# A two-layer hybrid backbone on one NeuronCore: the last scan group reordered, and seven attention steps placed beside the last projection tiles of the odd layer

## The chip, the cores and the metric

The program runs on one core of one Trainium2 chip. The metric is the device time of one execution in microseconds (us), lower is better. Engines are named as in the profile: PE is TensorE (matrix products), PEld its weight loads, DVE is VectorE, ACT is ScalarE, POOL is GpSimd, SP is SyncE, which here only issues transfers. Each engine works through its own list of instructions in order; the engines meet at semaphores.

## The reference, cut to what matters

256 latent tokens and 256 context tokens of width 1024 pass through two layers in fp32. The even layer mixes by a Fourier part and a bidirectional state-space scan (four groups of six heads, four chunks of 128 tokens); the odd layer mixes by attention. Each layer ends with a squared-ReLU MLP. The two places that the change touches:

```python
# even layer: per group of heads, over chunks of 128 tokens, in both directions
y = C_chunk @ entering_state * decay + (B C^T * decay_mask) @ (x * dt)

# odd layer
qw, kw, vw, qn, kn, vn = split(u @ w_in)           # 8 window heads over 2 shared k/v heads, 8 neighbourhood heads
q, k = rms_norm(q) * g, rms_norm(k) * g            # per head of 64
qw, kw = axial_rope(qw), axial_rope(kw)            # latent tokens, window heads alone
p = softmax([scores over 256 latent and 256 context keys, (window: sink)] + mask or bias)
out = concat(p_window @ vw, p_neighbour @ vn) @ w_out
```

## The kernel before, in words

**Order.** `script()` (L162) writes one list of steps, and every engine's block walks this same list and emits its own share of each step. So the order of the list is the order of work on every engine, and a step moved in it moves on all of them. `job()` (L376) gives every matrix product a PSUM bank (of 8) and keeps which semaphore count frees the bank's previous user; PE waits for that count (`emptied`) before it writes.

**Projection tiles.** A product by 128 columns of a weight is a step `gemm`. Every fp32 weight tile is loaded by SP into a ring of 4 slots, split by ACT into a rounded part (`high`, L1023: `w_hi`) and by DVE into the rest (`low`, L1393: `w_lo`), both done at the step of the tile two places ahead (`AHEAD = 2`). A tile is then 24 matmuls (8 pieces of the contraction by hi·hi, lo·hi, hi·lo), over 512 columns for k and v and 256 for q.

**Odd layer before.** `ODD` (L90) lists 18 tiles: v.0 to v.4, kw.0, kn.0 to kn.3, qw.0 to qw.3, qn.0 to qn.3. After tile n come, on the following places of the list: `hstat` of tile n-1 (PE sums squares over each head in a bank of `B_AUX`, ACT takes ln and exp), `hnorm` of tile n-2 (five DVE operations, L1821 to L1829; the second, L1823, is the last reader of the `hstat` bank), `rot` of tile n-3 for window heads (PE permutes, three DVE operations L1835 to L1838), `vtok` (PE transposes v, ACT copies), and `dup` (two PE products and two DVE copies that lay each shared key head twice, seven tiles behind kw.0).

**Attention before.** 16 steps i, for 8 pairs of heads t and two query halves. A step is: `S` (PE, four matmuls into two neighbouring banks), `max` (DVE adds mask or bias, reduces, negates; L1859 to L1870), `exp` (ACT, two exponentials that free the two banks, L1370, and for the window heads one for the sink, L1373), `scale` (DVE reciprocal and two multiplications, L1882 and L1886), `PT` (PE transposes the probabilities, ACT copies them, L1381), `O` (PE, L2386), and for every second step `ohi` (ACT) and `olo` (DVE) split the output. `S(0)` stands ahead of the last tile, everything else of attention behind it. `S` alternates between banks 4, 5 and 0, 1. Then come `grow` (transposes, L2199) and the tiles `outO`.

**Scan, last group before.** For each chunk: `seg` (ACT six Relu L1252 and one Exp L1255, DVE one product L1681, once for each direction f and b), `yoff` (PE L2164, DVE L1692, a sum L1697), `y` (PE: 24 products L2177, which wait for both `seg`, then six L2181 that add the `yoff` result and wait for DVE), `yt` (DVE adds the chunk to `mixF`, L1708). Beside them run the z tiles (DVE `gating`, L1405) and `mixsplit` f = 0 to 7 (DVE L1732 and L1734, or ACT for f below 2), which write the hi and lo operands of the pair of tiles outA 0 and outA 1. That pair (`pair_product`, L1920, 48 matmuls) waits at each of its eight pieces for the `mixsplit` of the piece.

Of the kernel before, what the change touches and what calls it, by code (L numbers as in the profile page):

```python
# [14 lines left out]
ALU = mybir.AluOpType  # L15
# [72 lines left out]

ODD_AT = {"qn": (768, SEQ), "kn": (1280, T), "qw": (0, SEQ), "kw": (512, T)}
ODD = [(kind, int(i), ODD_AT[kind][0] + P * int(i), ODD_AT[kind][1]) if kind != "v" else ("v", int(i), 640 if i == "0" else 1664 + P * int(i), T)  # L90
       for kind, i in (q.split(".") for q in ("v.0 kw.0 kn.0 kn.1 v.1 qw.0 qw.1 v.2 qw.2 qw.3 kn.2 qn.0 qn.1 kn.3 qn.2 qn.3 v.3 v.4").split())]
# [70 lines left out]
def script():  # L162
# [131 lines left out]
    for n in range(len(ODD) + 3):  # L294
        if n == len(ODD) - 1:
            s.append(("S", 0))
        if n < len(ODD):
            gemm(*ODD[n][:2])
        if n == len(ODD) - 1:
            s.append(("max", 0))  # L300

        behind = lambda back: [o[:2] for i, o in enumerate(ODD) if max(i, 1) == n - back]
        for back, stage in ((1, "hstat"), (2, "hnorm"), (3, "rot")):
            s.extend((stage,) + o for o in behind(back) if o[0] != "v" and (stage != "rot" or o[0][1] == "w"))
        s.extend(("vtok", o[1]) for o in behind(1) if o[0] == "v")
        s.extend(("dup",) for o in behind(7) if o[0] == "kw")
    n = len(ATTN)
    for j in range(-1, n + 1):
        for kind, i in (("S", j + 2), ("ohi", j - 2), ("max", j + 1), ("scale", j), ("olo", j - 2), ("exp", j + 1), ("PT", j), ("O", j - 1)):
            if kind in ("ohi", "olo"):  # L310
                if i >= 0 and i % 2 == 1:
                    s.append((kind, i // 2))
            elif 0 <= i < n and (kind, i) != ("max", 0):
                s.append((kind, i))
# [26 lines left out]
def trunk(nc, x, ctx, w_mod, vectors, w_ff1, w_ff2, w_in_even, w_dt, w_out_even, w_in_odd, rpb_na, w_out_odd,  # L341
# [45 lines left out]
    for st in steps:  # L387
# [93 lines left out]
        elif k == "cb":  # L481
            job(st, B_AUX[0])
        elif k == "hstat":
            job(st, B_AUX[n_aux % 2], freed=("hv_done", nk))
            n_aux += 1
        elif k == "yoff":
            for i, (q, none) in enumerate((("f", SCAN_F[0]), ("b", SCAN_B[0]))):
# [4 lines left out]
        elif k == "rot":  # L492
            job(st, B_Y)
        elif k == "dup":
            job(st + (0,), B_TR, freed=("kd_done", 1))
            job(st + (1,), B_TR, freed=("kd_done", 2))
        elif k == "S":
            for par in range(2):
                job(st + (par,), (B_SEG, B_GEMM[0])[st[1] % 2] + par)
        elif k == "PT":  # L500
            for par in range(2):
                job(st + (par,), (B_TR, B_AUX[0])[par], freed=("pT_done", 2 * st[1] + par + 1))
        elif k == "O" and st[1] % 2 == 0:
            t = st[1] // 2
            job(("Opair", t), (B_Y, B_AUX[1])[t % 2], freed=("split_done", 5 * KT + t + 1), filled=("pv_done", 4 * t + 4))
# [8 lines left out]
    with ExitStack() as stack:  # L514
# [505 lines left out]
        def _(act):  # L1020
# [39 lines left out]
            for st in steps:  # L1060
# [321 lines left out]
                elif k == "ohi":  # L1382
                    b = jobs[("Opair", st[1])][0]
                    act.wait_ge(*filled(("Opair", st[1])))
                    nc.scalar.activation(a_hi[:, st[1], 0:SEQ], ps[:, b, 0:SEQ], ACT.Copy).then_inc(signal(ohi_done), 1)


        @block.vector
        def _(dve):
# [51 lines left out]
            for st in steps:  # L1441
# [395 lines left out]
                    dve.wait_ge(*latest())  # L1837
                    v.tensor_tensor(x_, rp[:, 0, :], rp[:, 1, :], ALU.add).then_inc(signal(rope_done), 1)  # L1838
                elif k == "dup":
                    for q in range(2):  # L1840
                        b = jobs[st + (q,)][0]
                        dve.wait_ge(*filled(st + (q,)))
                        v.tensor_copy(kdup[:, q, :], ps[:, b, :]).then_inc(signal(kd_done), 1)
                elif k == "max":
                    i = st[1]
                    t, qt = ATTN[i]
# [57 lines left out]
        def _(pe):  # L1904
# [42 lines left out]
            for st in steps:  # L1947
# [391 lines left out]
                    mm(ps[:, b, 0:SEQ], cuts["perm"], ktile(*st[1:])[:, 0:SEQ], start=True, stop=True).then_inc(filling(st), 1)  # L2339
                elif k == "dup":  # L2340
                    pe.wait_ge(rope_done, rot_n[("rot", "kw", 0)] + 1)
                    for q in range(2):
                        b = jobs[st + (q,)][0]
                        if free_before[st + (q,)]:
                            pe.wait_ge(*emptied(st + (q,)))
                        mm(ps[:, b, :], cuts[f"dup{q}"], kT[:, 0, :], start=True, stop=True).then_inc(filling(st + (q,)), 1)
# [114 lines left out]
```

## Time and profile before

| what | us |
|---|---|
| runs, median of 3 (lowest to highest) | 1212.22 (1210.06 to 1213.14) |
| profiled execution, its own time | 1210.93 |
| its span, first to last instruction | 1209.1 |
| mean granted PE clock, share of full | 0.997 |
| busy: PE, PEld, DVE, ACT, POOL | 1162.3, 933.2, 841.0, 617.0, 84.4 |

The odd layer's tiles and attention stand from 855 to 993 us of the span, the last scan group from 341 to 394 us. Times in the rows are from the span's start. A busy share of PE near 1 means that matrix work follows without a gap; where it falls, another engine, or a semaphore, is late.

### The profile page before, as it was taken

What the parts mean: (1) busy time and instruction counts of PE and PEld (TensorE: products, weight loads), DVE (VectorE), ACT (ScalarE), POOL (GpSimd) and SP (SyncE); (2) the same over time, 40 slices, a digit from 0 to 9 for tenths busy, and PEclk for the clock granted to TensorE, in tenths of its full rate; (3) what the DMA queues carried; (4) which work ended last, traced back from release to release, by engine and by line L of the source; (5) the groups of instructions that cost most, each with busy time, mean ns of one, the idle gap of its engine ahead of it and who ended that gap; (6) DMA issues with size and microseconds to landing.
All of it is one profiled execution on the core that took longest, in us unless ns stands there. A gap on an engine that the chain in (4) does not pass through costs nothing.

```text
span 1209.1 us, 17206 instructions
## 1 busy us (share of the span) xinstructions
PE 1162.3 (96%) x6430; PEld 933.2 (77%) x6430; DVE 841.0 (70%) x1208; ACT 617.0 (51%) x1074; POOL 84.4 (7%) x73
## 2 busy tenths in 40 slices
PE   5999899999997999999999999999999899999998
PEld 3567677787776787887887887887877579998997
DVE  4563578887977566994783883897768977755555
ACT  5540384858665446721421421446844777744553
POOL 0000101010010024000000000034000004000000
PEclk9999999999999999999999999999999999999999
DMA  9856234332322233643543543542334004455554
GB/s 361 346 218 260 87 117 128 95 133 77 120 83 79 70 93 129 220 155 138 209 153 126 208 156 121 212 152 70 122 124 136 4 1 165 165 178 191 184 183 155
DMA packets 49893, 179.13 MB, mean 148 GB/s; under 512 B 5216, under 2 KB 7584, under 8 KB 47776
## 3 DMA queue, kind: packets, MB, share of 16 engines
q1 hardware_dynamic: 49536, 177.66, 42.5%
q8 instruction: 43, 0.70, 0.2%
q10 hardware_dynamic: 288, 0.56, 0.2%
q14 instruction: 26, 0.21, 0.1%
HBM read 177.05 MB, written 1.15 MB: 147 GB/s over the span
## 4 chain that ended last, share of the span: by engine, by line
PE 77%; DVE 9%; ACT 8%; DMA 3%; issue 2%; SPq 0%; DVEq 0%; ACTq 0%
PE ps L1913 50%; PE ps L1920 9%; PE ps L2207 6%; ACT ey L1252 3%; PE ps L2005 2%; DVE sm L1861 1%; DMA mhalf<-in_w_mod 1%; ACT ey L1255 1%; PE ps L1936 1%; DMA raw<-in_w_ff 1%; ACT cacc L1200 1%; PE ps L2181 1%; DVE prob L1886 1%; PE ps L2118 1%; DMA xload<-in_ctx 1%
## 5 line engine op out<-in xcount | busy, mean ns | idle before, releaser
L1396 DVE TENSOR_TENSOR w_lo<-raw,w_hi 128x1024 fp32r<-128x1024 f32 x206 | 263.1, 1278 | 90.8 <-ACT w_hi L1026 90.5
L1026 ACT ACTIVATE w_hi<-raw 128x1024 fp32r<-128x1024 f32 x206 | 216.8, 1053 | 198.8 <-DMA raw<-in_w_ff 155.5
L1913 PE MATMUL ps<-a_hi,w_hi 128*128 128x512 f32 (+1 forms) x820 | 299.3, 365 | 0.0
L1913 PE MATMUL ps<-a_hi,w_lo 128*128 128x512 f32 (+1 forms) x820 | 289.0, 352 | 0.0
L1913 PE MATMUL ps<-a_lo,w_hi 128*128 128x512 f32 (+1 forms) x820 | 288.7, 352 | 0.0
L1913 PEld LDWEIGHTS ps<-a_hi,w_hi 128*128 128x128 f32 x820 | 155.2, 189 | 24.9 <-issue 2.5
L1913 PEld LDWEIGHTS ps<-a_lo,w_hi 128*128 128x128 f32 x820 | 155.3, 189 | 23.1 <-issue 0.7
L1913 PEld LDWEIGHTS ps<-a_hi,w_lo 128*128 128x128 f32 x820 | 155.1, 189 | 21.4
L1913 PE MATMUL ps<-b_hi,w_hi 128*128 128x512 f32 x304 | 119.2, 392 | 0.0
L1913 PE MATMUL ps<-b_lo,w_hi 128*128 128x512 f32 x304 | 118.4, 390 | 0.0
L1913 PE MATMUL ps<-b_hi,w_lo 128*128 128x512 f32 x304 | 118.3, 389 | 0.0
L1773 DVE SCALAR_TENSOR_TENSOR macc<-mring,silc,macc 128x1536 f32<-128x1536 f32 x56 | 103.6, 1892 | 0.0
L1346 ACT ACTIVATE hr<-ps 128x512 f32<-128x512 f32 x30 | 17.9, 596 | 99.6 <-PE ps L1913 66.7
L1920 PE MATMUL ps<-a_hi,w_hi 128*128 128x512 f32 (+1 forms) x188 | 66.6, 354 | 1.6 <-DVE w_lo L1396 1.0
L1913 PEld LDWEIGHTS ps<-b_hi,w_hi 128*128 128x128 f32 x304 | 57.1, 188 | 14.3 <-DVE hT L1799 1.9
L1913 PEld LDWEIGHTS ps<-b_hi,w_lo 128*128 128x128 f32 x304 | 57.1, 188 | 12.0
L1913 PEld LDWEIGHTS ps<-b_lo,w_hi 128*128 128x128 f32 x304 | 57.1, 188 | 11.5
L1920 PE MATMUL ps<-a_hi,w_lo 128*128 128x512 f32 (+1 forms) x188 | 64.7, 344 | 0.0
L1920 PE MATMUL ps<-a_lo,w_hi 128*128 128x512 f32 (+1 forms) x188 | 64.7, 344 | 0.0
L1605 DVE SCALAR_TENSOR_TENSOR cacc<-cpad,vec,cacc 128x512 f32<-128x512 f32 x80 | 60.2, 752 | 5.5 <-ACT cacc L1200 0.7
L1252 ACT ACTIVATE ey<-ey,acum 128x128 f32<-128x128 f32 x192 | 59.3, 390 | 0.0
L1799 DVE SCALAR_TENSOR_TENSOR hT<-ps,mod,hT 128x256 f32<-128x256 f32 x64 | 28.0, 479 | 43.0 <-PE ps L1913 43.0
(289 smaller groups left out, 1766.5 us busy)
## 6 DMA issues: line engine op xcount, KB each, us to landing
raw<-in_w_ff SPq DMA_DIRECT2D x128, 512.0 KB, 3.5
mring<-in_w_mod SPq DMA_DIRECT2D x32, 768.0 KB, 5.2
raw<-in_w_in_even SPq DMA_DIRECT2D x36, 512.0 KB, 5.7
mring<-in_w_mod SPq DMA_DIRECT2D x16, 1024.0 KB, 6.4
ey<-acum_rows SPq DMA_DIRECT2D x32, 384.0 KB, 4.8
raw<-in_w_in_odd SPq DMA_DIRECT2D x18, 512.0 KB, 3.5
mhalf<-in_w_mod SPq DMA_DIRECT2D x16, 512.0 KB, 9.6
raw<-in_w_out_even SPq DMA_DIRECT2D x16, 512.0 KB, 3.5
```

Of the source, the lines that this page charges most:

```text
L1026: nc.scalar.activation(w_hi[:, u % RING, :, :], raw[:, u % RING, :, :], ACT.Copy).then_inc(hi_done, 1)
L1200: nc.scalar.activation(cacc[:, n % 2, :], ps[:, b, :], ACT.Identity, scale=convwT[:, CONV_W // 2, st[2]:st[2] + 1], bias=convbT[:, st[2]:s ...
L1252: nc.scalar.activation(ey[:, di, r, :], ey[:, di, r, :], ACT.Relu, scale=-1.0, bias=acum[:, st[3], head_col(st) + r:head_col(st) + r + 1]) ...
L1346: nc.scalar.activation(hr[:, m % 2, 0:ntok], ps[:, b, 0:ntok], ACT.Relu).then_inc(hr_done, 1)
L1396: v.tensor_tensor(w_lo[:, u % RING, :, :], raw[:, u % RING, :, :], w_hi[:, u % RING, :, :].bitcast(F32), ALU.subtract).then_inc(lo_done, 1)
L1605: v.scalar_tensor_tensor(out=acc, in0=cpad[:, n % 2, :, w:w + SEQ], scalar=convwT[:, w, t:t + 1], in1=acc, op0=ALU.mult, op1=ALU.add).then ...
L1773: ins = v.scalar_tensor_tensor(out=macc[i][:, :], in0=row, scalar=weight, in1=macc[i][:, :], op0=ALU.mult, op1=ALU.add)
L1799: ins = v.scalar_tensor_tensor(out=hs, in0=ps[:, b, SEQ * i:SEQ * i + SEQ], scalar=mod[:, L, 5 * KT + m, i:i + 1], in1=hs, op0=ALU.mult, o ...
L1913: ins = mm(out_ap, w_[:, n % RING, k, :], (x_[k][:, 0:ntok] if type(x_) is list else x_[:, k, 0:ntok]), start=(k == 0 and j == 0), stop=(k ...
L1920: ins = mm(outs[i], w_[:, tiles_[i] % RING, k, :], (x_[k][:, 0:ntok] if type(x_) is list else x_[:, k, 0:ntok]), start=(k == 0 and j == 0) ...
L2005: ins = mm(ps[:, LEAD_BANKS[i], 0:ntok], w_[:, slot + i, kk, :], x_[:, kk, c_:c_ + ntok], start=(kk == 0 and q == 0), stop=(kk == KT - 1 a ...
L2207: ins = mm(ps[:, B_TOK[q], :], x_[:, m, P * t:P * t + P], moving_rows(w_, u, half), start=(begin and j == 0), stop=(end and j == 2))
```

## The change

The last scan group is put in another order; the odd layer's tiles are put in another order, the first eight attention scores and seven full steps stand among its last tiles, `rot` stands ahead of `hstat` and `hnorm` once attention has begun, the last `hnorm` stands behind its attention step, and `dup` is split over two places.

```diff
 ODD: "v.0 kw.0 kn.0 kn.1 v.1 qw.0 qw.1
-      v.2 qw.2 qw.3 kn.2 qn.0 qn.1 kn.3 qn.2 qn.3 v.3 v.4"
+      kn.2 qw.2 qw.3 kn.3 qn.0 v.2 qn.1 v.3 qn.2 v.4 qn.3"
+FIRST_STEP, BESIDE = 11, 8
...
         for n in range(NCH):
-            if n < NCH - 1 and not (last and n == 0):
+            if n < NCH - 1 and not last:
                 s.append(("seg", g, "f", ch[n + 1]))
-            mixsplits(0, *((), (4,), (6, 7), ())[n])
             if n:
                 s.append(("yt", g, ch[n - 1]))
             s.append(("yoff", g, ch[n]))
+            mixsplits(0, *((), (2, 3), (6, 7), ())[n])
+            if last and n == 0:
+                s.append(("seg", g, "b", ch[1]))
             slot(2 + n)
-            if n < NCH - 1:
+            if last and 0 < n < NCH - 1:
+                s.append(("seg", g, "f", ch[n + 1]))
+            mixsplits(0, *((), (4,), (), ())[n])
+            if n < NCH - 1 and not (last and n == 0):
                 s.append(("seg", g, "b", ch[n + 1]))
             mixsplits(0, *((), (5,), (), ())[n])
             s.append(("y", g, ch[n]))
-            mixsplits(0, *((2, 3), (), (), ())[n])
...
+    def attend(j):
+        if j == BESIDE:
+            s.append(("S", j + 1))
+        if j < BESIDE:
+            order = [("S", j + 1), ("PT", j), ("max", j + 1), ("O", j - 1), ("exp", j + 1)]
+            if j >= 2 and j % 2 == 0:
+                order += [("ohi", j // 2 - 1), ("olo", j // 2 - 1)]
+        else:
+            order = [("S", j + 2), ("ohi", (j - 2) // 2), ("max", j + 1), ("scale", j), ("olo", (j - 2) // 2), ("exp", j + 1), ("PT", j), ("O", j - 1)]
...
+    for n in range(FIRST_STEP + len(ATTN) + 1):
+        j = n - FIRST_STEP
+        if 0 < j < BESIDE:
+            s.append(("scale", j))
         if n < len(ODD):
             gemm(*ODD[n][:2])
...
+        norms = [("hnorm",) + o for o in behind(2) if o[0] != "v"]
+        turns = [("rot",) + o for o in behind(3) if o[0] in ("kw", "qw")]
+        if j >= 0:
+            s.extend(turns)
+        s.extend(("hstat",) + o for o in behind(1) if o[0] != "v")
+        if j < BESIDE - 1:
+            s.extend(norms)
+        if j < 0:
+            s.extend(turns)
+        if j == 0:
+            s.append(("scale", j))
         s.extend(("vtok", o[1]) for o in behind(1) if o[0] == "v")
-        s.extend(("dup",) for o in behind(7) if o[0] == "kw")
+        for q in range(2):
+            s.extend(("dup", q) for o in behind(6 + q) if o[0] == "kw")
+        if j >= -1:
+            attend(j)
+        if j >= BESIDE - 1:
+            s.extend(norms)
...
         elif k == "hstat":
-            job(st, B_AUX[n_aux % 2], freed=("hv_done", nk))
+            job(st, B_AUX[n_aux % 2 if st[1:] != ("kn", 3) and st[1] != "qn" else 1], freed=("hv_done", nk))
...
         elif k == "S":
             for par in range(2):
-                job(st + (par,), (B_SEG, B_GEMM[0])[st[1] % 2] + par)
+                job(st + (par,), (B_SEG, B_GEMM[0])[st[1] % 2 if st[1] > BESIDE else 0] + par)
...
-            job(("Opair", t), (B_Y, B_AUX[1])[t % 2], ...)
+            job(("Opair", t), B_AUX[1] if t >= 4 and t % 2 == 0 else B_Y, ...)
...
+        o_hi = place("o_hi", [P, 4, SEQ], F32R, offset=hr_at)
+        o_lo = place("o_lo", [P, 4, SEQ], F32R, offset=hr_at + 4 * 4 * SEQ)
...
                 elif k == "S":
-                    if i == 0: pe.wait_ge(rope_done, len(rot_n))
-                    if t == 4: pe.wait_ge(qn_done, len(hn_n))
+                    if qt == 0 and t < 4: pe.wait_ge(rope_done, rot_n[("rot", "qw", t)] + 1)
+                    if qt == 0 and t >= 4: pe.wait_ge(qn_done, hn_n[("hnorm", "qn", t - 4)] + 1)
```

The buffers of probabilities and their transposes get other places in SBUF, the first four output pairs of attention get hi and lo buffers of their own (`o_hi`, `o_lo`), since `a_hi` is still read by the tiles, and `O` waits for the v tile that it needs and no longer for all five.

Written out, the list of the new order, one place of the odd layer a line (tile, then what follows it):

```
n=7   kn.2; hstat qw.1; hnorm qw.0; dup 0
n=8   qw.2; hstat kn.2; hnorm qw.1; rot qw.0; dup 1
n=9   qw.3; hstat qw.2; hnorm kn.2; rot qw.1
n=10  kn.3; hstat qw.3; hnorm qw.2; S0; max0; exp0
n=11  qn.0; rot qw.2; hstat kn.3; hnorm qw.3; scale0; S1; PT0; max1; exp1
n=12  scale1; v.2; rot qw.3; hstat qn.0; hnorm kn.3; S2; PT1; max2; O0; exp2
n=13  scale2; qn.1; hnorm qn.0; vtok 2; S3; PT2; max3; O1; exp3; ohi0; olo0
n=14  scale3; v.3; hstat qn.1; S4; PT3; max4; O2; exp4
n=15, 16  the same with qn.2 and v.4
n=17  scale6; qn.3; hnorm qn.2; vtok 4; S7; PT6; max7; O5; exp7; ohi2; olo2
n=18  scale7; hstat qn.3; S8; PT7; max8; O6; exp8
n=19  S9; S10; max9; scale8; exp9; PT8; O7; hnorm qn.3
n=20  S11; ohi3; max10; scale9; olo3; exp10; PT9; O8   (from here as before)
```

and of the last scan group (new): yoff(2), seg b(3), tile z 11, y(2), yt(2), yoff(3), mixsplit 2 and 3, seg f(0), mixsplit 4, seg b(0), mixsplit 5, y(3), yt(3), yoff(0), mixsplit 6 and 7, outA 0 (with outA 1), seg f(1), seg b(1), y(0). Before: yoff(2), tile z 11, seg b(3), y(2), mixsplit 2 and 3, seg f(0), mixsplit 4, yt(2), yoff(3), seg b(0), mixsplit 5, y(3), seg f(1), mixsplit 6 and 7, yt(3), yoff(0), outA 0, seg b(1), y(0). The number is the chunk.

## Rows read from the trace of the kernel before

**Rows 1.** The page's busy times: engine, busy us, share, instructions.
```profile
PE 1162.3 (96%) x6430; PEld 933.2 (77%) x6430; DVE 841.0 (70%) x1208; ACT 617.0 (51%) x1074; POOL 84.4 (7%) x73
```

**Rows 2.** Waits of PE, 320 to 400 us: total us, times, longest.
```profile
PE ps L2181 <- DVEq L1699: 5.1, 2, 4.2
PE ps L2177 <- DVE ey L1681: 1.4, 1, 1.4
```

**Rows 3.** Windows in the scan's last group: length, busy of each engine, clock, DMA.
```profile
370.00:375.00 5.00, 1.38 (x6) 1.38 (x7) 4.57 (x8) 4.94 (x12) 0.00 (x0) 0.87 0.28 112
375.00:380.00 5.00, 5.00 (x18) 3.49 (x17) 4.72 (x9) 3.22 (x7) 0.00 (x0) 0.79 0.00 0
```

**Rows 4.** Timeline of the last scan group: start, us, engine, line [idle before].
```profile
364.99 1.23 DVE L1396 TENSOR_TENSOR w_lo<-raw,w_hi 128x1024 fp32r<-128x1024 f32 x1 [0.16 <-DVE ycomb L1692]
365.00 0.84 ACT L1255 ACTIVATE ey<-ey 128x768 f32<-128x768 f32 x1
...
366.92 0.96 DVE L1681 TENSOR_TENSOR ey<-ey,cbm 128x768 f32<-128x768 f32 x1
...
367.98 0.43 DVE L1732 CAST a_hi<-mixF 128x512 fp32r<-128x512 f32 x1
...
369.17 0.43 DVE L1732 CAST a_hi<-mixF 128x512 fp32r<-128x512 f32 x1
...
373.62 1.65 PE L2181 MATMUL ps<-c,ycomb 128*128 128x128 f32 x6 [4.16 <-DVEq L1699]
```

**Rows 5.** The chain of waits: start, us, what. First the pair outA.
```profile
377.52 10.92 PE ps L1920 x48
...
877.19 5.48 PE ps L1913 x24
...
891.27 2.88 PE ps L1913 x24
...
895.01 5.47 PE ps L1913 x24
```

**Rows 6.** Window over the odd layer's tiles and attention, columns as Rows 3.
```profile
855.00:1020.00 165.00, 155.29 (x1100) 124.22 (x1099) 128.26 (x257) 107.97 (x225) 13.19 (x13) 1.00 0.27 89
```

**Rows 7.** Waits of PE, 855 to 1000 us.
```profile
PE ps L2370 <- DVE prob L1886: 4.8, 8, 1.2
PE ps L2346 <- DVE kdup L1843: 1.4, 1, 1.4
```

**Rows 8.** Timeline of DVE between two projection tiles.
```profile
885.09 1.22 DVE L1396 TENSOR_TENSOR w_lo<-raw,w_hi 128x1024 fp32r<-128x1024 f32 x1 [1.46 <-ACT w_hi L1026]
886.24 0.42 DVE L1821 TENSOR_TENSOR u<-nt 128x256 f32<-128x256 f32 x1
886.69 0.42 DVE L1823 SCALAR_TENSOR_TENSOR u<-ps,u 128x256 f32<-128x256 f32 x1
...
888.27 0.43 DVE L1835 TENSOR_TENSOR rp<-qT,c 128x256 f32<-128x256 f32 x1
```

**Rows 9.** Timeline of one attention step, all engines.
```profile
958.29 0.42 DVE L1859 TENSOR_TENSOR ps<-ps,c 128x256 f32<-128x256 f32 x1
...
960.28 0.16 DVE L1868 TENSOR_TENSOR sm<-vec,sm 128x2 f32<-128x2 f32 x1
...
961.28 1.09 PE L2370 MATMUL ps<-c,prob 128*128 128x128 f32 x8 [0.41 <-DVE prob L1886]
961.54 0.69 DVE L1859 TENSOR_TENSOR ps<-ps,bias 128x512 f32<-128x512 f32 x1
...
961.81 0.20 ACT L1373 ACTIVATE sm<-sm 128x2 f32<-128x2 f32 x1
...
963.33 1.13 PE L2361 MATMUL ps<-kT,qT 64*128 64x512 f32 x4
```

**Rows 10.** Timeline, step 9's scale on DVE, and grow on PE.
```profile
970.26 0.17 DVE L1882 RECIPROCAL sm<-sm 128x2 f32<-128x2 f32 x1
...
992.29 1.09 PE L2199 MATMUL ps<-c,mod 128*128 128x128 f32 x8
```

More of the change, by code:

```diff
@@ L90 @@
 ODD = [(kind, int(i), ODD_AT[kind][0] + P * int(i), ODD_AT[kind][1]) if kind != "v" else ("v", int(i), 640 if i == "0" else 1664 + P * int(i), T)
-       for kind, i in (q.split(".") for q in ("v.0 kw.0 kn.0 kn.1 v.1 qw.0 qw.1 v.2 qw.2 qw.3 kn.2 qn.0 qn.1 kn.3 qn.2 qn.3 v.3 v.4").split())]
+       for kind, i in (q.split(".") for q in ("v.0 kw.0 kn.0 kn.1 v.1 qw.0 qw.1 kn.2 qw.2 qw.3 kn.3 qn.0 v.2 qn.1 v.3 qn.2 v.4 qn.3").split())]
 NORM_FF0, NORM_MIX1, NORM_FF1 = ("norm", 0, "ff"), ("norm", 1, "mix"), ("norm", 1, "ff")
@@ L293, in script @@
     s += [NORM_FF0, ("lead", NORM_FF0), ("mlp", 0), NORM_MIX1, ("lead", NORM_MIX1)]
-    for n in range(len(ODD) + 3):
-        if n == len(ODD) - 1:
-            s.append(("S", 0))
+    def attend(j):
[7 more added lines that the diff above has]
+            order = [("S", j + 2), ("ohi", (j - 2) // 2), ("max", j + 1), ("scale", j), ("olo", (j - 2) // 2), ("exp", j + 1), ("PT", j), ("O", j - 1)]
+        for kind, i in order:
+            if kind in ("ohi", "olo"):
+                if j < BESIDE or j % 2 == 1:
+                    s.append((kind, i))
+            elif 0 <= i < len(ATTN):
+                s.append((kind, i))
@@ L297, in script @@
+    for n in range(FIRST_STEP + len(ATTN) + 1):
+        j = n - FIRST_STEP
+        if 0 < j < BESIDE:
+            s.append(("scale", j))
         if n < len(ODD):
             gemm(*ODD[n][:2])
-        if n == len(ODD) - 1:
-            s.append(("max", 0))
         behind = lambda back: [o[:2] for i, o in enumerate(ODD) if max(i, 1) == n - back]
-        for back, stage in ((1, "hstat"), (2, "hnorm"), (3, "rot")):
-            s.extend((stage,) + o for o in behind(back) if o[0] != "v" and (stage != "rot" or o[0][1] == "w"))
@@ L305, in script @@
-        s.extend(("vtok", o[1]) for o in behind(1) if o[0] == "v")
-        s.extend(("dup",) for o in behind(7) if o[0] == "kw")
[L307 to L314, printed above, removed]
@@ L316, in script @@
+        for q in range(2):
[4 more added lines that the diff above has]
+            s.extend(norms)
+    s += [("ohi", len(ATTN) // 2 - 1), ("olo", len(ATTN) // 2 - 1)]
     s += [("grow",), ("vprep", NORM_FF1)]
@@ L494, in trunk @@
         elif k == "dup":
-            job(st + (0,), B_TR, freed=("kd_done", 1))
-            job(st + (1,), B_TR, freed=("kd_done", 2))
+            job(st, B_TR, freed=("kd_done", st[1] + 1))
         elif k == "S":
             for par in range(2):
-                job(st + (par,), (B_SEG, B_GEMM[0])[st[1] % 2] + par)
+                job(st + (par,), (B_SEG, B_GEMM[0])[st[1] % 2 if st[1] > BESIDE else 0] + par)
         elif k == "PT":
@@ L504, in trunk @@
             t = st[1] // 2
-            job(("Opair", t), (B_Y, B_AUX[1])[t % 2], freed=("split_done", 5 * KT + t + 1), filled=("pv_done", 4 * t + 4))
+            job(("Opair", t), B_AUX[1] if t >= 4 and t % 2 == 0 else B_Y, freed=("split_done", 5 * KT + t + 1), filled=("pv_done", 4 * t + 4))
     steps_of = lambda kind: [q for q in steps if q[0] == kind]
@@ L620, in trunk @@
         vtok = place("vtok", [P, NCH, 5 * P])
+        vtok_end = at[0]
         at[0] = max(at[0], region + 2 * 16384)
@@ L628, in trunk @@
         bias = place("bias", [P, 2, 8, SEQ], offset=region + 16384)
-        prob = place("prob", [P, 3, 2, T], offset=region + 32768)
-        pT = place("pT", [P, 2, 2, T], offset=region + 32768 + 12288)
+        prob = place("prob", [P, 3, 2, T], offset=macc_at + 7680)
+        pT = place("pT", [P, 2, 2, T], offset=vtok_end)
+        assert vtok_end + 8 * 2 * T <= region + 16384
+        o_hi = place("o_hi", [P, 4, SEQ], F32R, offset=hr_at)
+        o_lo = place("o_lo", [P, 4, SEQ], F32R, offset=hr_at + 4 * 4 * SEQ)
         fin = place("fin", [P, 2, D], offset=out_at)
@@ L657, in trunk @@
         mix_hi = [mixE[:, 0, k, :] if k < 2 else a_hi[:, k, :] for k in range(KT)], [b_hi[:, k, :] for k in range(KT)]
+        attn_hi = [o_hi[:, k, :] if k < 4 else a_hi[:, k, 0:SEQ] for k in range(KT)]
+        attn_lo = [o_lo[:, k, :] if k < 4 else a_lo[:, k, 0:SEQ] for k in range(KT)]
         mix_lo = [mixE[:, 1, k, :] if k < 2 else a_lo[:, k, :] for k in range(KT)], [b_lo[:, k, :] for k in range(KT)]
@@ L732, in operands @@
                 return mix_hi[half], mix_lo[half]
+            if st[1] == "outO":
+                return attn_hi, attn_lo
             return a_hi, a_lo
@@ L1384, in _ @@
                     act.wait_ge(*filled(("Opair", st[1])))
-                    nc.scalar.activation(a_hi[:, st[1], 0:SEQ], ps[:, b, 0:SEQ], ACT.Copy).then_inc(signal(ohi_done), 1)
+                    nc.scalar.activation(attn_hi[st[1]], ps[:, b, 0:SEQ], ACT.Copy).then_inc(signal(ohi_done), 1)
         @block.vector
@@ L1839, in _ @@
                 elif k == "dup":
[L1840 to L1843, printed above, removed]
+                    b = jobs[st][0]
+                    dve.wait_ge(*filled(st))
+                    v.tensor_copy(kdup[:, st[1], :], ps[:, b, :]).then_inc(signal(kd_done), 1)
                 elif k == "max":
@@ L1890, in _ @@
                     b, _ = jobs[("Opair", t)]
-                    v.tensor_tensor(a_lo[:, t, 0:SEQ], ps[:, b, 0:SEQ], a_hi[:, t, 0:SEQ].bitcast(F32), ALU.subtract).then_inc(signal(split_done), 1)
+                    v.tensor_tensor(attn_lo[t], ps[:, b, 0:SEQ], attn_hi[t].bitcast(F32), ALU.subtract).then_inc(signal(split_done), 1)
                 elif k == "out":
@@ L2341, in _ @@
                     pe.wait_ge(rope_done, rot_n[("rot", "kw", 0)] + 1)
[L2342 to L2346, printed above, removed]
+                    b = jobs[st][0]
+                    if free_before[st]:
+                        pe.wait_ge(*emptied(st))
+                    mm(ps[:, b, :], cuts[f"dup{st[1]}"], kT[:, 0, :], start=True, stop=True).then_inc(filling(st), 1)
                 elif k == "S":
@@ L2351, in _ @@
                         pe.wait_ge(kd_done, 2)
-                        pe.wait_ge(rope_done, len(rot_n))
-                    if t == 4:
-                        pe.wait_ge(qn_done, len(hn_n))
+                    if qt == 0 and t < 4:
+                        pe.wait_ge(rope_done, rot_n[("rot", "qw", t)] + 1)
+                    if qt == 0 and t >= 4:
+                        pe.wait_ge(qn_done, hn_n[("hnorm", "qn", t - 4)] + 1)
                     for par in range(2):
@@ L2375, in _ @@
                     pe.wait_ge(pT_done, 2 * i + 2)
-                    if i == 0:
-                        pe.wait_ge(vtok_done, 5)
+                    if qt == 0:
+                        pe.wait_ge(vtok_done, 1 if t < 4 else t - 2)
                     if i % 2 == 0:
```

1 line of the change is left out of this document (removed).

## The prediction

> **What bounds the kernel now.** I read the page's busy times first, then PE's waits, then the windows and timelines of the two places that the change touches. PE is busy 96% of the span [rows 1], and its matmuls are the same before and after, so the change can only remove or add PE's empty time. The Trainium skill, page "Perfetto Trace Analysis", section "Identifying the Most-Contended Engine", says that matmul busy time is a poor measure because pipelined matmuls look smaller there, and prefers the weight loads' share, 77% here. In the odd layer's 165 us the busy times leave 9.7 us empty [rows 6]; counted by starts, with a product's tail taken as empty when the next one is late, I get 11.5 us. By the one the odd part could give at most 9.7, by the other 11.5; neither ceiling is what decides below.
>
> In the last scan group PE waits 5.1 us for the `yoff` result and 1.4 us for `seg` [rows 2], and then runs at 0.87 and 0.79 of its clock over two windows of 5 us [rows 3]: 0.13·5 + 0.21·5 = 1.7 us of PE time lost at the lower of its two levels, 1.2 GHz. In the odd layer it waits 4.8 us for `scale`, 1.4 for `dup` [rows 7], and less for ACT.
>
> **The scan's last group.** Why `y` of chunk 3 waits: DVE does tile z 11 (`low` from 364.99, `gating`), `seg` b (366.92), three `mixsplit`s and `seg` f(0) between, and only then `yt` and `yoff`; PE starts its six products at 373.62 after 4.16 us of nothing [rows 4]. In the new order DVE does, from 364.99: `seg` b 0.96 (ACT had the decay factors at 365.84 because it did z 11 first; now that step stands ahead of z 11 there too, and I put it at 363.2, 1.6 of `high` and tanh and the wait for the tile earlier), `low` 1.15, `gating` 0.65, `yt` 0.5, `yoff` 0.6: 368.85. `seg` is ready at 365.95, ahead of PE's 24 products, so the wait of 1.4 goes, and the six products start at 368.9 instead of 373.62, without the slow clock: they take 0.7 and the two `yoff` products after them 1.4. The pair outA 0 and 1 starts at 371.0; before, the chain has it from 377.52 for 10.92 us to 388.44 [rows 5].
>
> Late next is `mixsplit`, now behind `yoff`. One takes 1.19 (369.17 less 367.98 [rows 4]), a `seg` 0.96. DVE from 368.85: `mixsplit` 2, 3 to 371.2; `seg` f(0), `mixsplit` 4 to 373.3; `seg` b(0), `mixsplit` 5 to 375.4; `yt`, two `yoff` and their sum to 377.6; `mixsplit` 6, 7 to 378.8 and 380.0. PE asks for piece k at 371.0 + 0.7 + 1.37(k-1): piece 6 at 378.5, which waits 0.3, piece 7 at 380.2. The pair ends at 382.5 against 388.44: -5.9 us. The next `y`s need DVE after the residual of outA 0 and two `seg`s (384.5), just when PE is through the products before; I give 0 for that, and at worst one `seg`, 1.0. SP's fetch of the last decay rows waits for y(2) and the weight loads for their slots, as before: they move with PE. So -5.9, bounds -3 (two thirds of the `mixsplit` work coming late) and -7 (the waits and all of the clock, 5.1 + 1.4 + 1.7, less 1 for the wait that stays).
>
> **The odd layer, up to the first step.** Durations: a tile of 512 columns with start and small products 5.91 (895.01 to 900.92 in the chain, one 256-column tile less: 891.27 to 895.01 is 3.74 [rows 5]); `S` 1.06; `PT` and `O` together 2.05 (961.28 to 963.33); `max` from `S` to the bias 2.15 (958.29 to 960.44); `exp` with the sink 1.54 (to 962.01) [rows 9]; `low` 1.14, the first two operations of `hnorm` 0.87, all five 1.93, `rot` on DVE 1.14 as three operations of 0.34 to 0.45 [rows 8]; `high` 1.05, about as long as `low`.
>
> The `dup` waits go: the two halves now stand a tile apart, and kn.2 and qw.2 cover the copy. That is 1.4 by the waits [rows 7] and 3.0 by starts. From the first 512-column tile at 877.2 PE runs through n=7 to n=10 without a wait: 877.2 + 5.9 + 0.6 (`dup` 0), + 4.2 + 0.6 (`dup` 1), + 3.7, + 5.9 = 898.1; `S0` ends at 899.1. DVE is through `hnorm` of qw.2 at 898.9, so it is ready.
>
> Then comes the step that I take to be the dear one. In n=11 PE has qn.0 (2.9) and the permutation for qw.2: it is at `hstat` kn.3 at 902.5. This product is now put in the second bank of `B_AUX`, as that of qw.3 was, so it waits until L1823 of `hnorm` qw.3 has read that. And `hnorm` qw.3 stands on DVE behind `rot`, that behind `low`, that needs ACT's `high`, and ACT has `exp0` ahead of it, which needs `max0`: 899.1 + 2.15 + 1.54 + 1.05 + 1.14 + 1.14 + 0.87 = 907.0. PE stands 4.5 us; behind it in its list stand `S1` and `PT0`. `scale0` is behind the norm too (first half at 909.0), so `PT0` waits another 0.5 and ends at 910.0.
>
> n=12 has it again: v.2 and the permutation end at 915.9; DVE does `rot` qw.3 only after that permutation (917.1), then the first two operations of `hnorm` kn.3 at 512 columns, 0.7 each as the bias addition of that width [rows 9]: 918.5. `hstat` qn.0, in the same bank, waits 2.6. So 7.6 us at the entry, where before there was none.
>
> n=12 to n=17 then run on PE: `hstat`, `S2`, `PT1`, `O0` to 921.9; q units of 2.9 + 0.6 + 3.1 and v units of 5.7 + 0.2 + 3.1 give 928.5, 937.5, 944.1, 953.1; qn.3's tile ends at 956.2. Here the cover works: from the end of `S(j)` to `scale(j)` are 2.15 + 1.54 + 1.3 = 5.0 us plus up to 2 for the norm ahead of `max`, and PE has 6.4 or more of other work until `PT(j)`.
>
> **The seam.** With tiles gone, `S0` to `S8` share banks 4 and 5. `S6` ends at 951.1: `max6` 953.2, `exp6` 954.8, `scale6` 956.1, `low` 957.3, `hnorm` qn.2 959.2, `max7` 961.4, `exp7` frees the banks at 962.8. PE was ready at 960.1 for `S8`: 2.7. `olo2` waits for ACT behind `exp7`, so `scale7` starts at 963.7: `PT7` waits 0.8. Then `max8` to 967.1, `exp8` 968.5 (`S10` waits 0.8), `max9` to 969.8, `scale8` (`PT8` 0.8), `hnorm` qn.3 1.9, `max10` to 974.8. `scale9` starts there; before it started at 970.26 [rows 10], and from there on the order is the old one, paced by DVE, up to `grow` at 992.29. So `grow` comes at 996.8: **+4.5 us** for the odd layer. Bounds: if the waits at the entry are half of mine, +0.7, if none, -3.1; if each of the dozen handovers takes 0.3 more, +8.
>
> **The clock.** The only long stop of PE in the rows, 4.16 us, is followed by the lower level [rows 3, 4]. The new stop at 902.5 is as long, and I expect the fall there too: the price there was 1.7 us, and half of the products that would run slow (`hstat`, `S1`) are waited for by nothing else; +1.0. The Trainium skill, page "TensorE: Matmul & The Clock Gate", section "Part 1: The HAM clock gate", says that an idle PE falls to the half rate and work brings it back. By that rule the scan's repair keeps the full clock and the new stop loses it, which the sum has from the rows.
>
> **Sum.** 1210.9 (profiled execution) - 5.9 + 4.5 + 1.0 = 1210.5. The median of the runs is 1.3 above the profiled execution: **1211.8**. The moved buffers cost nothing: same shapes, same instructions.
>
> **Rivals.**
> *The entry does not stop PE* (0.25). For it: all DVE and ACT waits in this stretch are short now, and DVE has over 20% empty time [rows 6]. Against it: PE's list holds `hstat` ahead of `S1`, and the bank is one. With 1 us of stops at the entry instead of 7.6 and no slow clock: 1211.8 - 6.6 - 1.0 = 1204.2.
> *PE loses its clock in the entry and at the seam* (0.15), the slower side. The seam has 7 us of stops in 15. For it: after 0.9 + 1.4 + 4.2 us of stops within 10 us the clock fell in the scan. Against it: attention has 4.8 us of waits in eight pieces now and the clock is 1.00 over the stretch [rows 6, 7], and DVE paces the seam. Two full falls (3.4 in place of 1.0), and the longer chains behind slow `S` products, 1.5: 1215.7. It decides from the point where PE stands 4 us in one piece.
> *The scan gives half* (0.10): DVE's work before `mixsplit` 7 is unchanged, and if it ends at 383 instead of 380 the pair waits 3 us: 1214.8.
>
> **Chances.** Likeliest case 0.50, its own range 1208.6 to 1215. A measurement tells 0.3% (3.6 us) from no change. Faster by more (below 1208.6): the first rival's 0.24 and 0.03 of the likeliest: 0.27. Slower by more (above 1215.9): 0.08 of the clock case, 0.04 of the scan case, 0.06 of the likeliest: 0.18. Within: 0.55. Range for 8 in 10: 1204.0 to 1217.0, the low end just past the first rival, the high end past the clock case.
>
> **What would show it.** In the scan: no stop above 1.2 us, no window under full clock, pair outA from 371. In the odd layer: one stop of PE of 4 to 5 us on `hstat` (L2325), released by L1823, about 25 us after the first 512-column q/k/v tile; another of 2.6; no `dup` wait; a wait of 2.7 of `S8` for `exp7`. The prediction is wrong if PE passes n=11 without that stop, or if `scale` at n=12 to 17 is late.

## The result, and the profile after

| | before | after |
|---|---|---|
| median of the runs (10 each), us | 1210.38 | 1214.91 |
| lowest to highest, us | 1208.43 to 1213.14 | 1214.27 to 1216.81 |
| ratio, 95% interval | | 1.0040 [1.0030, 1.0051] |
| profiled execution, span in it, us | 1210.9, 1209.1 | 1214.3, 1212.5 |

The change makes the kernel slower by 0.40%, about 4.8 us by the ratio and 4.5 by the medians; the forecast was 1211.8, 0.4 us under the 1212.2 that it started from and no measurable difference. The scan gave what was worked out and the odd layer took twice what was worked out. The page's busy times [rows 1] are now:

```profile
PE 1163.9 (96%) x6430; PEld 932.3 (77%) x6430; DVE 840.9 (69%) x1208; ACT 617.5 (51%) x1074; POOL 85.5 (7%) x73
```

**Scan.** PE's longest wait from 320 to 400 us (total, times, longest), against [rows 2]; two more of 0.4 are left, one of them for `mixsplit`:

```profile
PE ps L2213 <- DVEq L1732: 1.7, 2, 0.9
```

Windows of the same stretch, against [rows 3]; columns are the window, its length, PE, PEld, DVE, ACT, POOL busy, granted clock, DMA share and GB/s:

```profile
370.00:375.00 5.00, 5.00 (x24) 4.11 (x23) 4.76 (x8) 4.94 (x13) 0.00 (x0) 1.00 0.04 14
375.00:380.00 5.00, 4.57 (x21) 3.46 (x20) 4.66 (x8) 0.59 (x1) 0.00 (x0) 1.00 0.00 0
```

The wait of 4.2 us and that for `seg` are gone, the clock stays at 1.00. The chain of waits of before, at the start and behind the pair outA, and then that of after:

```profile
343.58 1.94 PE ps L2137 x6
...
394.38 5.70 PE ps L1913 x25
```

```profile
342.21 1.94 PE ps L2169 x6
...
377.57 3.69 PE ps L1952 x15
387.21 10.92 PE ps L1945 x48
```

The tiles behind the pair outA start at 387.21. Before they started at 394.38, and there the chain's piece answering to 342.21 stood at 343.58, so 1.37 us of the difference were there beforehand, in these two executions: 7.17 - 1.37 = 5.8 us gained.

**Odd layer.** PE's waits from 855 to 1000, against [rows 7]:

```profile
PE ps L2357 <- DVE u L1856: 7.4, 2, 4.7
PE ps L2402 <- DVE prob L1918: 4.7, 6, 1.7
PE ps L2393 <- ACT prob L1403: 3.5, 2, 2.7
```

The `dup` wait is gone; `hstat` (L2357) stands twice for `hnorm`. Over the whole stretch of [rows 6] the clock is 0.97 where it was 1.00, and PE is busy for 149.4 us where it was 155.3. Five windows at the entry:

```profile
895.00:900.00 5.00, 1.02 (x7) 0.61 (x6) 2.59 (x5) 2.89 (x8) 0.00 (x0) 0.93 0.31 105
900.00:905.00 5.00, 4.33 (x8) 1.35 (x9) 2.76 (x10) 1.32 (x2) 0.00 (x0) 0.50 0.00 0
905.00:910.00 5.00, 5.00 (x25) 4.35 (x24) 3.15 (x10) 3.65 (x8) 0.00 (x0) 0.88 0.00 0
910.00:915.00 5.00, 2.37 (x11) 1.65 (x9) 3.64 (x7) 0.60 (x1) 0.00 (x0) 1.00 0.38 121
915.00:920.00 5.00, 4.90 (x26) 3.21 (x28) 3.69 (x8) 2.42 (x5) 0.00 (x0) 0.66 0.12 40
```

PE does 1 us of work in the first, then runs a whole window at 0.50, which is the lower level of 1.2 GHz, comes back to 2.4 GHz, stands again in the fourth and falls again. A window's time at 1.2 GHz is twice its length times what the clock lacks to 1: 0.7 + 5.0 + 1.2 and then 3.4, 10.3 us in all. The chain of waits shows what ran in it (start, us, what):

```profile
870.06 5.46 PE ps L1945 x24
...
891.47 1.11 PE ps L2393 x4
...
900.67 2.04 PE ps L2357 x2
902.72 2.01 PE ps L2393 x4
904.73 1.73 PE ps L2402 x8
...
915.77 1.36 PE ps L2393 x4
917.13 1.90 PE ps L2402 x8
919.02 1.42 PE ps L2418 x16
920.45 3.07 PE ps L1945 x24
...
995.89 1.02 PE ps L2231 x8
```

From the first 512-column tile (870.06) to `grow` (995.89) are 125.8 us; before, 877.19 [rows 5] to 992.36, 115.2:

```profile
992.36 1.02 PE ps L2199 x8
```

The odd layer costs 10.7 us. This distance, **D** below, is the trace's measure for the experiments. With the scan's 5.8 the net is +4.9; the medians say +4.5. The two profiled executions differ by 3.4, since after's was 1.4 us ahead before the scan group.

### The profile page after: what moved, and what is told of

It reads as the page before. It is cut to its first block, busy times and chain, and to the rows that moved or that the text cites. A ratio compares the mean times of both kernels' runs of the same rounds, so it can differ in the third digit from the quotient of the medians.

```text
span 1212.5 us, 17207 instructions
## 1 busy us (share of the span) xinstructions
PE 1163.9 (96%) x6430; PEld 932.3 (77%) x6430; DVE 840.9 (69%) x1208; ACT 617.5 (51%) x1074; POOL 85.5 (7%) x73
## 4 chain that ended last, share of the span: by engine, by line
PE 78%; DVE 8%; ACT 7%; DMA 3%; issue 3%; POOL 1%; POOLq 0%; SPq 0%; DVEq 0%; ACTq 0%
PE ps L1945 48%; PE ps L1952 9%; PE ps L2239 6%; ACT ey L1285 3%; PE ps L2037 2%; DMA mhalf<-in_w_mod 1%; ACT ey L1288 1%; PE ps L1968 1%; DVE sm L1893 1%; PE ps L2402 1%; PE ps L2393 1%; PE ps L2357 1%; PE ps L2418 1%; ACT cacc L1233 1%; PE ps L2150 1%
## 5 line engine op out<-in xcount | busy, mean ns | idle before, releaser
L1945 PE MATMUL ps<-a_hi,w_hi 128*128 128x512 f32 (+1 forms) x796 | 291.5, 366 | 0.0
L1945 PE MATMUL ps<-a_hi,w_lo 128*128 128x512 f32 (+1 forms) x796 | 282.1, 354 | 0.0
L1945 PE MATMUL ps<-a_lo,w_hi 128*128 128x512 f32 (+1 forms) x796 | 281.9, 354 | 0.0
L1945 PEld LDWEIGHTS ps<-a_hi,w_hi 128*128 128x128 f32 x796 | 150.5, 189 | 25.5 <-issue 2.6
L1945 PEld LDWEIGHTS ps<-a_lo,w_hi 128*128 128x128 f32 x796 | 150.6, 189 | 22.8 <-issue 0.7
L1945 PEld LDWEIGHTS ps<-a_hi,w_lo 128*128 128x128 f32 x796 | 150.4, 189 | 21.3
L1952 PE MATMUL ps<-a_hi,w_hi 128*128 128x512 f32 (+1 forms) x180 | 64.3, 357 | 0.7 <-DVE a_lo L1767 0.4
L1952 PE MATMUL ps<-a_lo,w_hi 128*128 128x512 f32 (+1 forms) x180 | 62.4, 347 | 0.0
L1952 PE MATMUL ps<-a_hi,w_lo 128*128 128x512 f32 (+1 forms) x180 | 62.4, 347 | 0.0
```

Source lines behind the costliest of these rows:

```text
L1945: ins = mm(out_ap, w_[:, n % RING, k, :], (x_[k][:, 0:ntok] if type(x_) is list else x_[:, k, 0:ntok]), start=(k == 0 and j == 0), stop=(k ...
L1952: ins = mm(outs[i], w_[:, tiles_[i] % RING, k, :], (x_[k][:, 0:ntok] if type(x_) is list else x_[:, k, 0:ntok]), start=(k == 0 and j == 0) ...
```

## The experiments

"Of before" and "of after" are the two kernels; each ratio is to runs of before taken beside that experiment (medians 1210.0 to 1210.6). Each time is a median of runs, and each D and each clock is from one profiled execution.

**Two parts alone.** The list of the scan's last group from after put into before, and the reverse.

```
 before.script(), group `last`: mixsplit/seg order of after     (e1)
 after.script(),  group `last`: mixsplit/seg order of before    (e2)
```

> The kernel before with the last scan group in the new order; the odd layer is untouched. Theory A (the scan's reordering gains 5.9 us and the odd layer alone loses): 1210.4 - 5.8 = 1204.6, no window under full clock between 340 and 400 us, pair outA about 5.8 us earlier than before. Rival B (the scan's gain is given back further down, since the last steps of the group or the weight loads catch up): 1209 to 1211, with new waits of PE between 390 and 440 us.

Measured: 1204.15, ratio 0.9947 [0.9933, 0.9960], clock 1.00 from 340 to 400, D 115.2.

> The changed kernel with the scan's last group in the old order. Theory A (both parts add up): 1214.9 + 5.8 = 1220.7, and 10.3 over the kernel before. Rival B: if the two parts share a cost (for instance the state of the clock), less than the sum, 1216 to 1218.

Measured: 1220.14, ratio 1.0083 [1.0069, 1.0097], D 125.8. Its odd layer is that of after, and its stops at the entry are the same, but the clock fell elsewhere: once at the entry (0.60 and 0.71 from 905 to 915) and once at the seam, behind the last tile (0.75 and 0.91 from 965 to 975), while the entry's second stop, of 2.73 us, was followed by full clock. A line of PE's timeline and two windows:

```profile
921.39 0.67 PE L2353 MATMUL ps<-sq,c 128*128 128x256 f32 x2 [2.73 <-DVE u L1852]
920.00:925.00 5.00, 3.60 (x30) 2.31 (x30) 4.56 (x8) 1.98 (x4) 0.00 (x0) 1.00 0.34 124
965.00:970.00 5.00, 3.14 (x12) 1.90 (x12) 3.02 (x8) 3.19 (x9) 0.00 (x0) 0.75 0.00 0
```

What follows: the parts add up, -0.53% (6.4 us) and +0.83% (10.0 us), and their sum is, within the intervals, the whole. The scan is not where the forecast failed.

**The stops stay, PE is kept busy in them (e3).** Same list; throwaway products into the bank of the next tile, which that tile overwrites.

```
 elif k == "hstat":
+    # ahead of hstat kn.3: 18, ahead of hstat qn.0: 10
+    pe.wait_ge(*emptied(next_tile))
+    pe.wait_ge(lo_done, unit[next_tile] + 1)
+    for _ in range(count):
+        mm(ps[:, bank_of_next_tile, :], w_hi[:, slot, 0, :], a_hi[:, 0, :], start=True, stop=True)
```

> The changed kernel; ahead of the products hstat kn.3 and hstat qn.0, for which PE waits 4.7 and 2.7 us, PE issues 18 and 10 extra matmuls of 512 columns whose result is thrown away (they go into the bank that the next tile overwrites). At 0.227 us each they take 4.1 and 2.3 us, less than the waits. Nothing else moves. Theory A (most of what I missed is PE's clock, which falls in the first stop and stays low through the products behind it, and again at the second): the clock stays at 1.00 between 890 and 925 us, and the time falls by 4 to 5 us to 1210 to 1211. Rival B (the clock costs no more than the 1.0 us of the prediction, and the rest of the loss is longer handovers between the engines): 1213 to 1215. Rival C (extra work on PE is never free): above 1215.

Measured: 1211.99, ratio 1.0014 [1.0006, 1.0023]. The chain:

```profile
872.28 5.46 PE ps L1945 x24
...
893.70 1.11 PE ps L2400 x4
...
902.81 1.12 PE ps L2364 x2
903.93 1.06 PE ps L2400 x4
905.00 1.02 PE ps L2409 x8
...
918.38 3.06 PE ps L1945 x24
...
961.41 1.88 PE ps L2409 x8
963.29 1.86 PE ps L2425 x16
...
995.41 1.02 PE ps L2231 x8
```

`hstat` still comes 9.1 us behind `S0` (after: 9.2), so the dependency is untouched; but it takes 1.12 instead of 2.04, `S1` and `PT0` likewise, and the q tile behind `O0` starts 24.7 instead of 29.0 us behind `S0`. So 4.3 us of the entry were the clock, with work added and none removed. At the seam, untouched by this edit, a fall that after's trace does not have (e2's has it) took part of it back: `PT7` and `O6` 1.88 and 1.86 instead of 1.09 and 1.02. D 123.1.

**Filler at the seam too (e10).** As e3, and ahead of `S8` four products on the operands of step 0, into a bank that is written afresh later.

```
 elif k == "S":
+    if i == BESIDE:
+        pe.wait_ge(*emptied(("S", i + 1, 0)))
+        for _ in range(4):
+            mm(ps[:, bank_of_S9, :], qT[0:HD, 0, 0:P], kT[0:HD, 0, :], start=True, stop=True)
```

> The changed kernel with the 18 and 10 throwaway products at the entry as before and 4 more (64x512, operands of step 0, into a bank that is written afresh later) ahead of step 8's scores, so that TensorE stands neither at the entry nor long at the seam. Theory A (the clock is the missing term, and the rest of the odd layer came out as worked): clock 1.00 in every 5 us from 885 to 1000; probability turn 7 and output 6 back from 1.88 and 1.86 to 1.09 and 1.02 us, so 1.6 us less than the 1211.99 of the kernel with fillers at the entry alone: 1210.4, and from the first 512-column tile to the projection's start 121.5 us, against 115.2 of before and the 119.7 worked out without a clock term. Rival B (at the seam VectorE sets the pace and TensorE's clock is hidden there): 1211.5 to 1212, though the clock reads 1.00.

Measured: 1210.92, ratio 1.0006 [0.9997, 1.0015]; the clock is 1.00 in every window from 885 to 1000. The chain:

```profile
871.80 5.46 PE ps L1945 x24
...
902.33 1.13 PE ps L2364 x2
903.45 1.06 PE ps L2404 x4
904.51 1.02 PE ps L2413 x8
...
914.79 1.06 PE ps L2404 x4
915.85 1.02 PE ps L2413 x8
916.87 1.03 PE ps L2429 x16
917.90 3.06 PE ps L1945 x24
...
961.24 1.02 PE ps L2413 x8
962.26 1.02 PE ps L2429 x16
...
993.56 1.02 PE ps L2231 x8
```

D is 121.8, 1.4 less than e3 and 4.1 less than after, and the ratio is 0.34% under after's, 4.1 us. Expected from the clock were 121.5 and 1210.4. The time alone (1.1 us under e3, between the two theories, with overlapping intervals) would not decide; D and the two durations do.

**The stops made shorter, three ways.** e5: `exp0` behind the weight split of qn.0 only. e6: at the entry `rot` behind `hnorm`. e4: e5's edit, and `rot` qw.2 and qw.3 behind `max` 1 and 2.

```
 in script(), place n of the list, j = n - 11              (e4 and e5)
         if n < len(ODD):
             gemm(*ODD[n][:2])
+        if j == 0:
+            s.append(("exp", 0))
 in attend()
-            elif 0 <= i < len(ATTN):
+            elif 0 <= i < len(ATTN) and (kind, i) != ("exp", 0):
                 s.append((kind, i))
+            if kind == "max" and 0 <= j < 2:                (e4 alone)
+                s.append(("rot", "qw", j + 2))
 in script()                                              (e4 and e6)
-        if j >= 0:
-            s.extend(turns)
...
-        if j < 0:                                           (e6 alone)
-            s.extend(turns)
+        s.extend(turns)
```

> The changed kernel with another order at the entry alone: exp0 stands behind the weight split of tile qn.0 (ACT does the split first), and the rotations of qw.2 and qw.3 stand behind max1 and max2, so that hnorm is ahead of them. Theory A (the two stops come from what is queued ahead of hnorm on DVE and ACT, and the slow clock from the stops): the stop of 4.7 us becomes about 1, that of 2.7 about 1, the clock stays up, and the time falls by about 10 us to 1204 to 1206. Rival B (the entry is limited by the attention chain S, max, exp, scale, whatever the order): the stop moves from hstat to PT0 and PT1 and the time falls by less than 4 us, to above 1211.

> The changed kernel; exp0 alone stands behind the weight split of tile qn.0. Theory A (the first stop is made of what ACT does ahead of the split: max0 waits for nothing, exp0 is 1.5 us, and the split 1.05 is then already done; and PE's clock falls only after a stop as long as 4 us): the first stop goes from 4.7 to about 2 us, the second stays at 2.7, the clock stays up between 890 and 925 us; 2.7 us of stop and about 4 of clock: 1208 to 1209. Rival B (the clock falls for the sum of the stops, not for the long one): it still falls at the second stop, and the time is 1211 to 1212.

> The changed kernel; at n=11 and n=12 the rotation stands behind hnorm instead of ahead of it, nothing else. Theory A (rot ahead of hnorm costs 1.1 us in the first stop and nearly all of the second, where rot also waits for its product behind tile v.2): first stop 3.6, second under 1.2. The first stop is then near the length at which the clock fell: 1211 to 1212 with the clock falling once, 1208 if it doesn't. Rival B (rotations ahead of norms cost nothing, the stops are made by low alone): 1214 to 1215.

| | median | ratio | D | PE's two stops for `hstat` | clock 895 to 920 |
|---|---|---|---|---|---|
| after | 1214.91 | 1.0040 [1.0030, 1.0051] | 125.8 | 4.66, 2.73 | 0.93 0.50 0.88 1.00 0.66 |
| e5 | 1210.42 | 1.0008 [0.9996, 1.0019] | 123.8 | 2.20, 2.73 | 0.97 0.69 1.00 0.84 0.82 |
| e6 | 1210.92 | 1.0010 [1.0001, 1.0019] | 122.6 | 3.96, 1.36 | 1.00 0.66 1.00 1.00 1.00 |
| e4 | 1208.81 | 0.9983 [0.9973, 0.9993] | 120.0 | 1.32, 0.91 | 1.00 1.00 1.00 1.00 1.00 |

The `hstat` stops of e5 and e4 in the timeline of PE, the idle time in brackets:

```profile
899.69 2.04 PE L2359 MATMUL ps<-sq,c 128*128 128x512 f32 x2 [2.20 <-DVE u L1858]
913.16 1.02 PE L2359 MATMUL ps<-sq,c 128*128 128x256 f32 x2 [2.73 <-DVE u L1858]
```

```profile
898.72 1.10 PE L2359 MATMUL ps<-sq,c 128*128 128x512 f32 x2 [1.32 <-DVE u L1858]
908.73 0.67 PE L2359 MATMUL ps<-sq,c 128*128 128x256 f32 x2 [0.91 <-DVE u L1858]
```

What follows: the stops come, as forecast, from what stands ahead of the norm that frees the bank (`exp0` on ACT, the weight split and `rot` on DVE), and reordering removes them. e4 stops a third time, 1.85 us for `rot` ahead of `O0`, and still keeps its clock. None of the three came out as expected: e4 came to 1208.81, between the 1204 to 1206 of its theory A and the 1211 of B, since the third stop and the seam's fall were not in the expectation; e5 came to 1210.42, again between its two theories, with the clock falling twice at the entry; e6 came out just under its 1211 to 1212. A stop of 2.20 us (e5) was followed by the fall as well as one of 4.66, so "4 us in one piece" is not the point from which it decides. All three lost at the seam what after's trace does not (0.82 to 0.84 in two windows, or 0.66 in one). e5's profiled execution is one of its long ones (1213.95; its runs reach from 1208.59 to 1214.71), so its D is for that execution.

**The seam (e7, and with e4 e8).** One step fewer beside the tiles, so that `S8` uses the two banks of the finished tiles and need not wait for `exp7`.

```
-FIRST_STEP, BESIDE = 11, 8
+FIRST_STEP, BESIDE = 11, 7
-                if j < BESIDE or j % 2 == 1:
+                if j < BESIDE or (j > BESIDE and j % 2 == 1):
-  (B_SEG, B_GEMM[0])[st[1] % 2 if st[1] > BESIDE else 0] + par
+  (B_SEG, B_GEMM[0])[(st[1] + 1) % 2 if st[1] > BESIDE else 0] + par
```

> The changed kernel with the old attention order one step sooner (BESIDE 7): S8 goes to banks 0 and 1 and doesn't wait for exp7, max8 stands ahead of scale7, and hnorm of qn.2 behind max7. The entry is as in the changed kernel. Theory A (the seam costs its latency since S has a single pair of banks and hnorm is ahead of max): step 9's scale comes about 2 us earlier after the last tile, the wait for exp7 of 2.7 goes, 1213. Rival B (DVE paces the seam, so whatever PE is given sooner is worth nothing): 1214.5 to 1215.5 with DVE busy over 4.7 of 5 us in the windows of the seam.

Measured: 1214.16, ratio 1.0028 [1.0016, 1.0040], D 126.5.

> The entry order of e4 (exp0 behind the split, rotations behind max) together with the seam order of e7. If the two add up: 1208.8 - 2 = 1207, and 1205 if with shorter stops at the seam the clock no longer falls there, as it did in e4 (two windows at 0.83). That would still be above the 1204.2 of the scan's part alone: the odd part would then be at best neutral. Rival: the seam isn't reached any sooner and the time is that of e4, 1208.8.

Measured: 1208.02, ratio 0.9982 [0.9973, 0.9991], D 118.9. The waits for `exp` went, but `hstat` qn.3 then stood for DVE, and e7's seam shows:

```profile
960.00:965.00 5.00, 3.63 (x10) 1.16 (x10) 3.60 (x8) 0.89 (x2) 0.00 (x0) 0.76 0.00 0
965.00:970.00 5.00, 3.57 (x24) 3.09 (x24) 4.79 (x13) 3.46 (x9) 0.00 (x0) 0.50 0.00 0
970.00:975.00 5.00, 5.00 (x36) 2.78 (x34) 4.05 (x10) 1.81 (x5) 0.00 (x0) 0.71 0.00 0
```

2.4 + 5.0 + 2.9 = 10.3 us at the lower level, where after had none: about what was won in waits was given to the clock. The entry of e7 is that of after and spent 6.9 us at the lower level (0.66, 0.98, 0.67), not 10.3. The seam's gain cannot be told from nothing by these runs (the intervals of e7 and after, and of e8 and e4, overlap).

**The best version (e9).** e1, and of the odd layer's edits only the `dup` products a tile apart.

```
-        s.extend(("dup",) for o in behind(7) if o[0] == "kw")
+        for q in range(2):
+            s.extend(("dup", q) for o in behind(6 + q) if o[0] == "kw")
```

> The kernel before with the new order of the scan's last group (1204.15 us) and, of the odd-layer edits, only the cut of the key copies in two (one bank filled per tile, instead of both in a row with a copy between them). Theory A (a wait of TensorE for VectorE inside the projection tiles is on the path that sets the end): the 1.44 us stand for the first key copy goes, the 0.8 us one for the token-major values may stay: 1202.7 us, 1202.0 if both go. Rival B (the stretch after the tiles is set by VectorE's queue, which has the same work to do in the same order): 1204.1. Either way no stand over 1.5 us and a granted clock of 1.00 through the tiles.

Measured: 1201.12, ratio 0.9927 [0.9913, 0.9940], D 113.5. Its waits of PE from 855 to 1005:

```profile
PE ps L2372 <- DVE prob L1889: 4.8, 8, 1.2
PE ps L2348 <- ACT vtok L1248: 0.8, 1, 0.8
```

Two more, 1.3 for `vtok` and 1.1 for `exp`, stand in before too. Only the 1.4 for `kdup` is gone, D is 1.7 shorter than e1's. The medians differ by more, 3.0 us, with ratios of separate sets of runs whose intervals overlap; the mechanism vouches for 1.7. This version is faster than before by 0.73%, and its median is the lowest here; against e1 the gain rests on D and on the wait that is gone.

## Why the prediction failed

- *Scan, -5.9:* right. Measured by the trace 5.8, by e1 0.53%. No stop above 0.9 us, no window below full clock, as foretold.
- *`dup`, 1.4 by the waits:* right in size (e9: it goes, D -1.7).
- *Entry, one stop of 4.5 and one of 2.6:* right. 4.66 and 2.73, both released by the second operation of `hnorm` (L1856, L1823 of before), the first 30.6 us behind the first 512-column tile, where 29.8 was worked out. The further 0.5 for `PT0` did not come. The rival that had PE pass the entry is refuted.
- *Seam, 2.7, 0.8, 0.8, 0.8:* right in place and roughly in size. 2.65 for `exp7`, then 0.40, 0.86, 0.96 in PE's timeline and 1.74 ahead of `PT9`.
- *Odd layer without clock, +4.5:* D would be 119.7. e10 has 121.8 with the clock at 1.00. The 2.1 us more stand in thirds: 0.7 before the first stop's end, 0.7 more up to the end of `O0` (46.1 behind the first tile, worked out 44.7), 0.7 more up to `grow`. I take them for handovers of a few tenths that the sum left out, which no run tests; they lie inside the bound of +8 that they were given.
- *Clock, +1.0:* **this step failed, and it was 4.1.** It assumed one fall, priced as in the scan, with half of the slow products "waited for by nothing else". There were two falls, and nothing of the slow products was hidden: after less e10, in the order of the chain, `hstat` kn.3 0.91, `S1` 0.95, `PT0` 0.71, then `S2` 0.30, `PT1` 0.88, `O0` 0.39: 4.1 us, the 4.1 by which D shrinks. PE's list is in order and its next tile is ready; behind a stop every product that runs slow pushes all work behind it. That `S1`'s own result is wanted late doesn't matter when PE itself is the bound [rows 1].
- *The rival with a lost clock in the entry and at the seam* (1215.7) was nearest the time. In after's trace both falls lie at the entry, and its seam, with a stop of 2.65, stayed at 1.00; in e2's, with the same odd layer and the same D, one lies at each place, as the rival had it. Its condition of 4 us in one piece is refuted by e5.

By the trace, the change of -0.4 that was forecast became +4.9: 3.1 from the clock, 2.1 from the odd layer without it, 0.1 from the scan. The forecast time is off by only 3.1 us, and 1214.91 still lies in the range of the likeliest case (1208.6 to 1215), because the median of three from which it was reckoned, 1212.2, stood 1.8 above before's median of ten, 1210.38: that is luck and no merit of the sum.

The Trainium skill, page "TensorE: Matmul & The Clock Gate", section "Part 1: The HAM clock gate", says that an idle PE falls to the half rate; e3 and e10 agree, since work of no use ended the falls. It also says there, of a kernel's start, that one and the same kernel shows different numbers of slow matmuls from run to run. The falls here vary in place between after and e2, which have the same odd layer, started 6 us later in e2; whether e5's spread of 6 us comes from that is not shown, since only one of its runs was profiled.

What stays open: why the seam's stop of 2.6 us for `exp7`, the same to 0.03 us in after, e2, e3, e4, e5 and e6, is followed by the lower level in five of them and not in after, and why the entry's second stop of 2.73 is followed by it in after, e5 and e7 and not in e2. How often the clock falls in a usual execution of after is not shown either: the one profiled was the shortest of ten, with a mean clock of 0.996, and seven of the ten show 0.991 to 0.994. And the last 2.1 us of the odd layer were located, but not tested one by one.

## What to carry to other kernels

On an engine that is busy 96% of the time and works its list in order, price a slow clock at the full extra time of every product that runs in it, and for each new stop that it can fall behind, not once for the group. Before overlapping two phases, look at what the last reader of a shared bank stands behind on its own engine: here moving three steps, `exp0` on ACT and two `rot` on DVE, was worth 6 us (e4). It did not make the overlap pay: e4 is at 1208.81, and e1, with the odd layer of before, at 1204.15. Take a change apart: its scan order and the cut of `dup` in two were the gain (-0.73%), the rest of the odd layer's edits together the loss; its new tile order and its attention steps beside the tiles were not tested apart.

## What was unexpected of the hardware

- Throwaway products made a kernel faster: 28 of 512 columns at the entry and 4 at the seam, 1214.91 to 1210.92 us, with all real work the same.
- The fall does not go by the length of the last stop alone. Stops of 2.20 and 2.73 us (e5) were followed by 1.2 GHz; stops of 1.32, 0.91 and 1.85 (e4) were not; those of 2.73 at the entry and of 2.65 at the seam went either way.
- It comes back within one or two windows of 5 us and can be lost again: after was at 0.50 in 900 to 905, at 1.00 in 910 to 915, at 0.66 in 915 to 920.
